# Third mixer of a two-block transformer: the causal mask written into the score bank by ScalarE for twelve units, instead of added by a matmul

## The reference

```python
def masked_softmax(s, mask):
    return jax.nn.softmax(jnp.where(mask, s.astype(jnp.float32), NEG), axis=-1)   # NEG = -1e30

# nsa_attention, for the queries at positions tpos (8 query heads, 2 key heads, head size 64)
p_c = masked_softmax(q @ k_cmp * scale, cmp_end <= tpos) * m_c        # 15 compressed blocks of keys
p_s = masked_softmax(q @ k_slc * scale, (kpos <= tpos) & selected)    # selected blocks of 64 keys
p_w = masked_softmax(q @ k_win * scale, (diff >= 0) & (diff < 512))   # window of 512
o_a = gates[0] * p_c @ v_cmp + gates[1] * p_s @ v_slc + gates[2] * p_w @ v_win
# forgetting_attention (8 heads)
p_f = masked_softmax(q @ k * scale + c[tpos] - c[kpos], kpos <= tpos)
```

## Time and profile before

| | us |
|---|---|
| three runs, median | 1188.25 (1187.95 to 1188.26) |
| the profiled execution, its own time | 1188.23 |
| its span | 1186.4 |
| PE busy | 1179.0 (99%) |
| PE weight loads | 1010.1 (85%) |
| DVE busy | 746.8 (63%) |
| ACT busy | 622.7 (52%) |
| POOL busy | 45.4 (4%) |

### The profile page before, as it was taken

One profiled execution on the slowest core, in us unless ns is written; L12 is line 12 of the kernel. 1 busy time (PEld: TensorE's weight loads), 2 busy tenths in 40 slices (PEclk: granted clock), 3 DMA queues, 4 the chain that ended last, 5 costly groups with the idle time before them and its releaser, 6 DMA issues.

```text
span 1186.4 us, 16292 instructions
## 1 busy us (share of the span) xinstructions
PE 1179.0 (99%) x6443; PEld 1010.1 (85%) x6443; DVE 746.8 (63%) x990; ACT 622.7 (52%) x937; POOL 45.4 (4%) x64
## 2 busy tenths in 40 slices
PE   9999999999999999999999999999999999999998
PEld 8888899898888889989888888888888888888887
DVE  6689655547866865455696445447977575454456
ACT  5654544344567553444456434436877774344445
POOL 2000000000000000000000000001102010000000
PEclk9999999999999999999999999999999999999999
DMA  8565554655644365556555565554543346655550
GB/s 285 204 213 204 197 195 162 210 185 190 211 151 139 120 230 195 178 186 204 178 168 180 185 212 178 180 175 148 182 144 105 116 126 211 211 179 180 175 178 36
DMA packets 119963, 210.78 MB, mean 178 GB/s; under 512 B 8320, under 2 KB 67024, under 8 KB 119888
## 3 DMA queue, kind: packets, MB, share of 16 engines
q1 hardware_dynamic: 119344, 209.35, 53.4%
q10 hardware_dynamic: 544, 0.40, 0.1%
HBM read 208.68 MB, written 1.05 MB: 177 GB/s over the span
## 4 chain that ended last, share of the span: by engine, by line
PE 97%; DVE 1%; ACT 0%; DMA 0%; issue 0%; POOL 0%; DVEq 0%; ACTq 0%; POOLq 0%
PE psum L341 25%; PE psum L343 24%; PE psum L342 24%; PE psum L349 4%; PE psum L350 4%; PE psum L355 4%; PE psum L1520 2%; PE psum L1484 2%; PE psum L1507 1%; PE psum L853 1%; PE psum L540 1%; PE psum L1475 1%; DMA x<-in_x 0%; PE psum L2927 0%; PE psum L1494 0%
## 5 line engine op out<-in xcount | busy, mean ns | idle before, releaser
L293 DVE TENSOR_TENSOR wl<-ring,wh 128x2048 fp32r<-128x2048 f32 x131 | 300.0, 2292 | 261.8 <-ACT wh L284 261.7
L284 ACT ACTIVATE wh<-ring 128x2048 fp32r<-128x2048 f32 x131 | 250.6, 1916 | 215.5 <-PE psum L343 215.5
L341 PE MATMUL psum<-wh,xT_high 128*128 128x512 f32 (+4 forms) x576 | 224.8, 390 | 0.0
L343 PE MATMUL psum<-wh,xT_low 128*128 128x512 f32 (+4 forms) x576 | 218.9, 380 | 0.0
L342 PE MATMUL psum<-wl,xT_high 128*128 128x512 f32 (+4 forms) x576 | 218.2, 379 | 0.0
L341 PE MATMUL psum<-wh,hidT_high 128*128 128x512 f32 (+2 forms) x472 | 178.8, 380 | 0.2
L342 PE MATMUL psum<-wl,hidT_high 128*128 128x512 f32 (+2 forms) x472 | 178.0, 379 | 0.0
L343 PE MATMUL psum<-wh,hidT_low 128*128 128x512 f32 (+2 forms) x472 | 177.9, 378 | 0.0
L341 PE MATMUL psum<-xT_high,wh 128*128 128x256 f32 x480 | 136.0, 283 | 0.0
L343 PE MATMUL psum<-xT_high,wl 128*128 128x256 f32 x480 | 135.8, 283 | 0.0
L342 PE MATMUL psum<-xT_low,wh 128*128 128x256 f32 x480 | 135.8, 283 | 0.0
(11 more groups left out here) (331 smaller groups left out, 1478.0 us busy)
## 6 DMA issues: line engine op xcount, KB each, us to landing
ring<-in_mlp_w_up SPq DMA_DIRECT2D x32, 1024.0 KB, 5.7
ring<-in_mlp_w_down SPq DMA_DIRECT2D x32, 1024.0 KB, 5.0
ring<-in_ffn_wg SPq DMA_DIRECT2D x44, 512.0 KB, 4.0
ring<-in_ffn_wu SPq DMA_DIRECT2D x44, 512.0 KB, 5.0
ring<-in_ffn_wd SPq DMA_DIRECT2D x22, 1024.0 KB, 5.0
ring<-in_ple_w_gate SPq DMA_DIRECT2D x12, 1024.0 KB, 5.1
ring<-in_w_in SPq DMA_DIRECT2D x10, 1024.0 KB, 5.1
ring<-in_a_w_in SPq DMA_DIRECT2D x8, 1024.0 KB, 9.7
```

What stands on the lines that cost most here:

```text
L284: K.nc.scalar.activation(parts_of(K, n)[0][:, 0:w], K.ring[:, n % SLOTS, 0:w], ACT.Copy).then_inc(K.high_ready, 2)
L293: K.nc.vector.tensor_tensor(low[:, 0:w], K.ring[:, n % SLOTS, 0:w], high[:, 0:w].bitcast(F32), ALU.subtract).then_inc(K.low_ready, 2)
L341: nc.tensor.matmul(out, x[0], w[0], start=start, stop=False)
L343: return nc.tensor.matmul(out, x[1], w[0], start=False, stop=stop)
```

## The change

Units of selected and window attention get a `fill`, the causal mask in float32. A unit is now `filled` only if its `prior` has a `fill` too; so units 16 and 17, behind the compressed 14 and 15, stay on the matmul path, and so do 0 and 1, which are first in their banks. ACT's list has the step `"mask"` in twelve new places, for units 2 to 11, 18 and 19, each right behind the exponentials of the last unit but one. DVE's and PE's lists are as before.

```diff
@@ Units.__init__
-        self.filled = [u["fill"] is not None and p is not None for u, p in zip(units, self.prior)]
+        self.filled = [u["fill"] is not None and p is not None and units[p]["fill"] is not None
+                       for u, p in zip(units, self.prior)]
@@ nsa_mixer, the units of kinds slc and win
-                u.update(k=K.keys2[:, first_key + kv, :, 0:size], v=[values(vc + kv * HD)] * 2)
+                u.update(k=K.keys2[:, first_key + kv, :, 0:size], fill=K.causal[:, SEQ - size:SEQ], v=[values(vc + kv * HD)] * 2)
@@ nsa_mixer, act_steps
         yield "scores", 0
+        yield "mask", 2
         yield "sigmoid",
         yield "scores", 1
+        yield "mask", 3
         yield "turn", 0
...
         yield "scores", 6
+        yield "mask", 8
         yield "turn", 4
         yield "scores", 7
+        yield "mask", 9
         yield "high", 13, 0
...
         yield "scores", 17
+        yield "mask", 19
         yield "high", 17, 1
```

More of the change, by code:

```diff
@@ L2578, in act_steps @@
         yield "scores", 2
+        yield "mask", 4
         yield "high", 11, 0
@@ L2582, in act_steps @@
         yield "scores", 3
+        yield "mask", 5
         yield "scores", 4
+        yield "mask", 6
         yield "turn", 2
@@ L2586, in act_steps @@
         yield "scores", 5
+        yield "mask", 7
         yield "turn", 3
@@ L2600, in act_steps @@
         yield "scores", 8
+        yield "mask", 10
         yield "take", 3, 0
         yield "scores", 9
+        yield "mask", 11
         yield "turn", 7
@@ L2625, in act_steps @@
         yield "scores", 16
+        yield "mask", 18
         yield "turn", 15
         yield "scores", 17
+        yield "mask", 19
         yield "high", 17, 1
```

## The result

| | before | after |
|---|---|---|
| median of 18 runs each, us | 1188.04 | 1190.45 |
| all runs, us | 1187.85 to 1188.38, and one of 1676.17 | 1190.26 to 1190.78 |
| span of the profiled execution, us | 1186.4 | 1188.7 |
| PE busy / ACT busy, us | 1179.0 / 622.7 | 1179.4 / 628.3 |

The ratio after to before is 1.002, with a 95% interval of 1.0013 to 1.0028. The one long run of before, 1676.17 us, is explained by nothing on record, is left out of the ratio, and doesn't move the median. So the change made the kernel slower by 2.41 us.

What follows compares the result with a forecast made beforehand. The prediction took PE, 97% of the chain, as the bound: -1.32 us of removed matmuls, +0.22 of added ones and +3.6 of waits for late ACT work make +2.5, so 1190.8 us, range 1189.4 to 1191.9.

Steps and rivals of the forecast that it cites:

- PE's removed and added work: Third mixer: twelve window-mask matmuls go, -1.32 us; two half-bank matmuls come at units 0 and 1, +0.22 us.
- place 1: Near 854 us: unit 2's fill delays the gates' exponential, then DVE's low weight half, so PE waits 0.42 us.
- What a fill costs ACT: ACT, third mixer: six small fills cost 0.45 us each, six large ones 0.67, in all 6.7 us.
- Places 4 and 5: PE's transposes at 873.1 and 875.7 us wait for ACT's late copies of turned probabilities: 0.3 and 1.1 us.
- Place 6: PE waits for unit 10's fill until about 880.5 us: 0.6 us.
- Places 2, 3, 7: PE waits for unit 6's fill, 0.21 us; a Silu near 869, 0.1; a late ACT copy near 888, 0.3.
- Place 8: Near 917.9 us: unit 19's fill pushes squares, DVE and an ACT copy, so PE waits 0.5 us.
- the prediction's signs: PE's lateness against before: near +0.4 us at 857, +1.6 at 876, +2.2 at 890, +2.5 from 918, then constant.
- turn 6 doesn't wait: Rival: the copy near 875.7 us releases PE in time, giving +1.4 us, 1189.7 us; chance 0.22.
- ACT's pauses take up the fills: Rival: the fills fit into ACT's idle time, leaving only -1.10 us, 1187.1 us; chance 0.06.
- all of ACT's 6.7 us arrive: Rival: all the time the fills cost ACT reaches PE, giving 1193.9 us; chance 0.03.
- a wait costs PE more than its length: Rival: each of eight PE restarts loses a 0.11 us slot or a copy misses its place: +0.9, 1191.6 us; chance 0.15.

Runs made afterwards that it cites:

- e1: Kernel before with PE's part alone: no fill or mask matmul in the twelve units, units 0 and 1 keep their additional matmul; 1186.99 us, -1.02 against before.
- e2: Kernel before with ACT's part alone: twelve mask copies at the fills' places into an unread SBUF tile, PE unchanged; 1190.55 us, +2.54 against before.
- e9: Changed kernel without the two added half-bank matmuls of units 0 and 1; 1190.45 us, +2.37 against before.
- e7: Changed kernel with fills read from the bfloat16 window mask instead of the float32 causal mask; 1190.43 us, +2.38 against before.
- e11: Changed kernel with unit 2's fill one operation later in ACT's list, behind the gates' exponential; 1190.24 us, +2.17 against before.
- e5: Changed kernel with unit 9's fill moved behind ACT's copy of unit 5's turned probabilities; 1189.82 us, +1.77 against before.
- e10: Kernel before with only the fills of units 18 and 19, mask matmuls for all others; 1188.35 us, +0.27 against before.
- e6: Changed kernel with each fill's copy done once more ahead of it, into an unread SBUF tile; 1194.10 us, +6.05 against before.

## Why the prediction was right

The forecast was +2.5 us, 1190.8; measured were +2.41 and 1190.45. The ratio of 1.002 lies on the edge of 0.2% itself, so on which side it came out is chance. Step by step:

- **PE's removed and added work (-1.32 + 0.22).** Sizes right: e1 gives -1.02 where their sum is -1.10, and the added pairs stand 0.11 us apart. But none of it has a part in the result, as e2 shows, whose PE has the old list and resumes at the same times. For the +0.22 and the masks of units 2 and 3 it is the wait of place 1 that follows them, at a time set by DVE. The prediction had this in its own lines ("not late itself (0.22 - 0.22), waits until 854.60") and still booked the 0.22 as a cost of its own. The sum survives since the wait was reckoned to the same fixed time; e9's expectation, which took the term by itself, missed for that reason.
- **What a fill costs ACT (0.45 and 0.67).** Measured 0.47 and 0.68; fill durations 388 and 602 ns, against 381 and 602; float32 reads no slower (e7).
- **Place 1.** 0.42 us forecast and measured; the chain is confirmed by e11, which gave back 0.24 where some 0.2 was expected.
- **Places 4 and 5.** Turn 5 was to start at 873.1 and turn 6 at 875.7; they start at 872.96 and 875.53, that is 873.14 and 875.71 with the 0.18 us by which this execution was early. The 1.1 us of place 5 hold (1.05, of which moving fill 9 takes its share of 0.6 away, e5). Place 4 cost more than its 0.3: 0.47, because PE came there less late than reckoned (0.24 instead of 0.3) and because 873.1 less 872.46 + 0.3 is 0.34, which the prediction rounded down.
- **Place 6.** 880.4 (880.5 in its sum); measured 880.23 + 0.18 = 880.41. The wait is 0.66, as the unrounded terms of its sum give it.
- **Places 2, 3, 7.** Their waits are in the weight-load view, of the kinds forecast, with 0.16, 0.10 and 0.21 us against 0.21, 0.1 and 0.3; no run tried them singly.
- **Place 8.** 917.9; measured 917.70 + 0.18 = 917.88. e10 has it alone: +0.27, that is a wait of 0.49 less two masks.
- **Constant afterwards.** The same key-tile wait stands 2.28 later, and the span ends 2.3 later.

PE's lateness can be followed from one matmul to its like in the other trace: the difference of the starts plus 0.18. A wait is the growth of the lateness since the place above, plus 0.11 for each mask that PE dropped in between (ahead of place 1 two masks and the two added matmuls cancel):

| place | start before | start after | lateness | wait forecast | wait measured |
|---|---|---|---|---|---|
| 1 | 854.41 | 854.65 | 0.42 | 0.42 | 0.42 |
| 2 | 863.33 | 863.40 | 0.25 | 0.21 | 0.16 |
| 3 | 869.42 | 869.48 | 0.24 | 0.1 | 0.10 |
| 4 | 872.57 | 873.10 | 0.71 | 0.3 | 0.47 |
| 5 | 874.20 | 875.67 | 1.65 | 1.1 | 1.05 |
| 6 | 879.39 | 881.30 | 2.09 | 0.6 | 0.66 |
| 7 | 885.98 | 887.99 | 2.19 | 0.3 | 0.21 |
| 8 | 915.66 | 917.94 | 2.46 | 0.5 | 0.49 |

The lateness is that of the prediction's signs (0.4, 1.6, 2.2, 2.5). The waits come to 3.56 against 3.5 to 3.6, although those of places 2, 4 and 7 are off by 0.05 to 0.18. That they cancel is not all luck: each wait is reckoned up to a release by ACT or DVE, so an error in PE's own lateness at one place is largely taken back at the next.

The rival that turn 6 doesn't wait (0.22) is refuted by its 0.86 us pause; that ACT's pauses take up the fills (0.06), by e2; that all of ACT's 6.7 us arrive (0.03), by the 2.41. The rival that a wait costs PE more than its length (0.15) is not borne out: the eight waits, each taken from ACT's end plus 0.17, give +2.5 us with PE's -1.10, without anything on top, and the trace has 2.46. The prediction's chance for slower is 0.504 by its own terms, where it says 0.51. The Trainium skill (Perfetto Trace Analysis, Identifying the Most-Contended Engine) judges Scalar by its occupancy. ACT's occupancy, 52% before, reads 53% for a kernel that ACT made slower; so for a stage with its own dependencies the mean of the whole span was no guide here.

## What to carry to other kernels

In this kernel, moving work from the engine that bounds it to one that is half idle paid only where the second had nothing behind the new operation that the first would soon need. So put the operation behind the result that is awaited, and not at the earliest moment at which it can run. For each moved operation, list the next results that the bounding engine takes from that queue with their margins, and add up lateness over consecutive ones. What is cut ahead of a wait with a fixed end is worth nothing (e2, e9).

## What the runs showed that was not expected

- PE with 1.10 us less work resumed at the same times as PE with its old list (the change and e2), once ACT was late. Likewise two matmuls less ahead of a wait gave nothing (e9, 1190.45 us with and without them), though PE makes up 97% of the chain that ended last.
- Doubling the fills cost 3.64 us more where the first set had cost 2.41: with the margins used up, each further microsecond of ACT (5.2 by the estimate of the expectation) arrives at PE to about 70%.
- A copy of 256 or 512 elements a partition into PSUM took the same 0.38 to 0.39 and 0.60 us from bfloat16 and float32 sources; the same copies into SBUF took 0.42 and 0.63 us (e2, at the places of the change's fills, and e6, means of six each). In e2 the operation behind such a copy started no later for it than behind the change's fill (872.46 and 872.45). Directly behind the SBUF copies of e6 the fills themselves took 0.37 and 0.58 us. The SBUF copies of e6:

```profile
L1562 ACT ACTIVATE aside<-causal 128x512 f32<-128x512 f32 x6 | 3.8, 631 | 0.2
...
L1562 ACT ACTIVATE aside<-causal 128x256 f32<-128x256 f32 x6 | 2.5, 418 | 0.2
```
